# Half-frequency Fourier mixer and another order of the modulation blocks in a two-layer diffusion backbone

## The reference, cut to what matters

```python
def ada_modulation(cond, w_mod, b_mod):            # w_mod is 1024 x 6144, one for each layer
    m = jax.nn.silu(cond) @ w_mod + b_mod
    return jnp.split(m, N_MOD, axis=-1)

def fourier_mix(u):                                 # u is real: 256 tokens x 4 groups of 128 channels
    b, n, _ = u.shape
    ug = u.astype(jnp.float32).reshape(b, n, FNET_GROUPS, FNET_GROUP_DIM)
    y = jnp.fft.fft2(ug, axes=(1, 3), norm='ortho').real
    return y.reshape(b, n, FNET_WIDTH).astype(u.dtype)

def even_layer(...):
    sh1, sc1, g1, sh2, sc2, g2 = ada_modulation(c[:, None, :], mod_w, mod_b)
    h = modulate(rms_norm(x, norm_mix), sh1, sc1) @ w_in
    u, q, k, v = jnp.split(h, cuts, axis=-1)
    q = rms_norm(split_heads(q, NA_HEADS, NA_HEAD_DIM), q_gain)
    k = rms_norm(split_heads(k, NA_HEADS, NA_HEAD_DIM), k_gain)
    o_lat = jnp.concatenate([fourier_mix(u), neighbourhood_attention(q, k, v, kc, vc, rpb)], axis=-1)
    x = x + g1 * (o_lat @ w_out)
    x = x + g2 * swiglu(modulate(rms_norm(x, norm_ffn), sh2, sc2), w1, w3, w2)
```

## Time and profile before

| | us |
|---|---|
| device time, median of 3 runs | 1917.22 (1913.81 to 1921.48) |
| device time of the profiled execution | 1918.17 |
| its span, first to last instruction | 1916.0 |
| PE busy | 1820.9 (95%) |
| start of the input projection | 46.76 |
| its end, start of the transposes of q and k | 152.53 |
| start of the Fourier pass | 158.85 |
| end of the Fourier pass | 179.68 |
| start of the output projection | 267.97 |

### The profile page before, as it was taken

One profiled execution on the slowest core, in us unless ns is written; L12 is line 12 of the kernel. 1 busy time (PEld: TensorE's weight loads), 2 busy tenths in 40 slices (PEclk: granted clock), 3 DMA queues, 4 the chain that ended last, 5 costly groups with the idle time before them and its releaser, 6 DMA issues.

```text
span 1916.0 us, 25182 instructions
## 1 busy us (share of the span) xinstructions
PE 1820.9 (95%) x8938; PEld 1416.2 (74%) x8938; DVE 1262.6 (66%) x1321; ACT 1002.5 (52%) x1088; POOL 313.0 (16%) x584
## 2 busy tenths in 40 slices
PE   3999889999999989797999999999999999999998
PEld 1775444888888876465888888888888888888886
DVE  2433633433333344644998988989889899898997
ACT  3322322422222221363677767777777777776774
POOL 6888821011010224101000000000000000000000
PEclk8999999999999999897999999999999999999999
DMA  9575952032322151502699998999989999998994
GB/s 369 203 280 174 374 211 88 33 121 77 112 86 93 72 201 58 162 4 88 262 368 356 354 374 336 367 351 359 371 345 363 348 357 370 350 358 347 366 366 184
DMA packets 72373, 481.80 MB, mean 251 GB/s; under 512 B 8368, under 2 KB 11568, under 8 KB 17456
## 3 DMA queue, kind: packets, MB, share of 16 engines
q1 hardware_dynamic: 68720, 470.82, 64.7%
q0 software_dynamic: 2448, 7.61, 1.3%
q10 hardware_dynamic: 1136, 2.47, 0.4%
HBM read 473.55 MB, written 7.32 MB: 251 GB/s over the span
## 4 chain that ended last, share of the span: by engine, by line
PE 91%; DMA 4%; DVE 2%; issue 1%; ACT 1%; SPq 0%; POOL 0%; DVEq 0%; ACTq 0%
PE bank L1020 32%; PE bank L1034 16%; PE bank L752 12%; PE bank L722 4%; PE bank L605 3%; PE bank L781 3%; PE bank L769 3%; DMA ring<-in_od_mod 3%; PE bank L818 2%; PE bank L547 2%; PE bank L993 2%; DMA ring<-in_ev_mod 1%; PE bank L1003 1%; PE bank L589 1%; PE bank L571 1%
## 5 line engine op out<-in xcount | busy, mean ns | idle before, releaser
L1772 DVE TENSOR_TENSOR rest<-ring,WR 128x2048 fp32r<-128x2048 f32 x336 | 758.5, 2289 | 79.4 <-ACT WR L1344 78.6
L1344 ACT ACTIVATE WR<-ring 128x2048 fp32r<-128x2048 f32 x336 | 631.6, 1917 | 49.0 <-DMA ring<-in_experts 47.9
L1020 PE MATMUL bank<-WR,xer 128*128 128x512 f32 x1792 | 580.9, 396 | 0.7 <-DVE s5v L1933 0.7
L1020 PEld LDWEIGHTS bank<-WR,xer 128*128 128x128 f32 x1792 | 337.7, 188 | 68.7 <-issue 0.8
L1020 PE MATMUL bank<-rest,xer 128*128 128x512 f32 x896 | 350.5, 391 | 0.0
L1034 PE MATMUL bank<-WR,heTr 128*128 128x512 f32 x896 | 281.9, 392 | 0.0
L752 PE MATMUL bank<-hTr,WR 128*128 128x512 f32 x672 | 207.3, 390 | 0.0
L1034 PEld LDWEIGHTS bank<-WR,heTr 128*128 128x128 f32 x896 | 168.2, 188 | 34.2
L1020 PEld LDWEIGHTS bank<-rest,xer 128*128 128x128 f32 x896 | 169.3, 189 | 32.7
L1034 PE MATMUL bank<-rest,heTr 128*128 128x512 f32 x448 | 174.5, 389 | 0.0
L1624 DVE TENSOR_TENSOR rest<-ring,WR 128x2048 fp32r<-128x2048 f32 (+2 forms) x38 | 80.3, 2116 | 124.5 <-ACT WR L1269 124.3
(11 more groups left out here) (336 smaller groups left out, 2179.7 us busy)
## 6 DMA issues: line engine op xcount, KB each, us to landing
ring<-in_experts SPq DMA_DIRECT2D x336, 1024.0 KB, 4.8
ring<-in_ev_mod SPq DMA_DIRECT2D x24, 1024.0 KB, 7.4
ring<-in_od_mod SPq DMA_DIRECT2D x24, 1024.0 KB, 8.8
ring<-in_ffn_up SPq DMA_DIRECT2D x22, 1024.0 KB, 6.9
ring<-in_ffn_down SPq DMA_DIRECT2D x12, 768.0 KB, 5.2
ring<-in_ev_in SPq DMA_DIRECT2D x8, 1024.0 KB, 9.8
ring<-in_ev_out SPq DMA_DIRECT2D x4, 1024.0 KB, 9.9
ring<-in_od_out SPq DMA_DIRECT2D x4, 1024.0 KB, 12.9
```

The source lines that it names most:

```text
L1020: mm = pe.matmul(bank[m % 2][:, :], xer[:, i, 4 * kh + k, :], w[j][:, 512 * k:512 * k + 512], start=(kh == 0 and k == 0 and x == 0), stop= ...
L1344: act.activation(part(0, h), ring[:, h % HALVES, :], ACT.Copy).then_inc(split_hi, 1)
L1772: dve.tensor_tensor(part(1, h), ring[:, h % HALVES, :], part(0, h).bitcast(F32), ALU.subtract).then_inc(split_lo, 1)
```

## The change

The Fourier mixer computes frequencies 0 to 128 only. The token transform is 258 columns wide (129 cosines, 129 sines). The channel transform puts its two products of 129 columns side by side in one bank instead of summing them; ACT copies the second one to `TQ`, and DVE writes the sum for frequencies 0 to 128 and the difference, read backwards, for 129 to 255. POOL's head 2 waits for `four_o` = 8 (DVE's last write) instead of `four_b` = 8. The table `dft` shrinks from 1280 to 772 columns.

`norm_turn(0)` follows block 1 instead of block 2. ACT takes the squares first; it issues `s5b` and `s5c` behind them when the second half of block 1 is there, and `dft` after the modulated input. ACT's first split of `ev_in` no longer waits for `coef`.

Blocks 4 to 18, fifteen of them, stand at fixed chunks of `w_in_even()` (`UNDER_IN`), 19 and 20 between transposes of q and k, 21 in the Fourier pass, and 22 and 23 in steps 0 and 2 of the attention. The order and the slots of the loads follow. The projection uses banks 4, 5, 6 and 2, so that bank 7 is free for the odd layer's blocks. `modulation_row(1)` moves behind group 9 and `modulation_turn(1)` ahead of group 12. The splits of the third and fourth slot are issued one group later for the first half.

```diff
@@ tables @@
-LATE = 12
-         + [("in", 0), ("mod", 4), ("in", 1), ("mod", 5), ("mod", 6), ("in", 2), ("mod", 7), ("mod", 8),
-            ("in", 3), ("mod", 9), ("mod", 10), ("mod", 12), ("mod", 11)]
-         + [("mod", s) for s in range(13, 24)])
-EARLY_SLOT = [0, 1, 2, 0, 1, 0, 2, 0, 0, 1, 0, 0, 2, 0, 0, 1, 0] + [2, 1] * 5 + [2]
+         + [("in", 0), ("mod", 4), ("mod", 5), ("mod", 6), ("in", 1), ("mod", 7), ("mod", 8), ("mod", 9),
+            ("in", 2), ("mod", 10), ("mod", 11), ("mod", 12), ("mod", 13), ("in", 3)]
+         + [("mod", s) for s in range(14, 24)])
+EARLY_SLOT = [0, 1, 2, 0, 1, 2, 0, 2, 0, 2, 2, 1, 2, 1, 1, 0, 1, 0, 1, 2, 1, 2, 1, 2, 1, 2, 0, 1]
+UNDER_IN = {(0, 2): 4, (0, 3): 5, (0, 5): 6, (0, 7): 7, (5, 2): 8, (5, 7): 9, (7, 4): 10, (8, 7): 11, (9, 5): 12,
+            (10, 2): 13, (12, 0): 14, (13, 4): 15, (14, 1): 16, (14, 6): 17, (15, 3): 18}
+UNDER_TURN = {0: 19, 2: 20}
+UNDER_FOUR = {1: 21}
+UNDER_ATTN = {0: 22, 2: 23}
@@ fourier() on PE @@
-                            mm = pe.matmul(bank[4 + u % 2][:, :], hn[:, 0, 2 * s + k, g * P:(g + 1) * P],
-                                           dft[:, k * 512:(k + 1) * 512], start=(k == 0), stop=(k == 1))
+                            mm = pe.matmul(bank[4 + u % 2][:, 0:2 * HALF_F], hn[:, 0, 2 * s + k, g * P:(g + 1) * P],
+                                           dft[:, 2 * HALF_F * k:2 * HALF_F * (k + 1)], start=(k == 0), stop=(k == 1))
-                            mm = pe.matmul(bank[6 + v % 2][:, 0:SEQ], dft[:, 1024 + k * P:1024 + (k + 1) * P],
-                                           T1[:, v % 2, k * SEQ:(k + 1) * SEQ], start=(k == 0), stop=(k == 1))
+                            mm = pe.matmul(bank[(6, 2)[v % 2]][:, 256 * k:256 * k + HALF_F],
+                                           dft[:, 4 * HALF_F + k * P:4 * HALF_F + (k + 1) * P],
+                                           T1[:, v % 2, HALF_F * k:HALF_F * (k + 1)], start=True, stop=True)
@@ head of the PE program @@
-                if s == 2:
+                if s == 1:
                     norm_turn(0)
@@ ACT @@
-            act.wait_ge(half_landed[0], 16)
-            act.dma_start(tail[:, 0:512], a["s5b"]).then_inc(s5_raw, 16)
-            act.dma_start(tail[:, 512:1024], a["s5c"]).then_inc(s5_raw, 16)
-            act.dma_start(dft, a["dft"]).then_inc(dft_landed, 16)
             squares(0)
+            act.wait_ge(half_landed[3], 16)
+            act.dma_start(tail[:, 0:512], a["s5b"]).then_inc(s5_raw, 16)
+            act.dma_start(tail[:, 512:1024], a["s5c"]).then_inc(s5_raw, 16)
...
+            split_in(0)
             act.wait_ge(coef_ready, 1)
             act.wait_ge(ht_act, 4)
-            split_in(0)
...
+            act.dma_start(dft, a["dft"]).then_inc(dft_landed, 16)
             for x in range(1, 4):
                 split_in(x)
...
+                    act.wait_ge(four_b, v + 1)
+                    if v >= 2:
+                        act.wait_ge(four_o, v - 1)
+                    act.activation(TQ[:, v % 2, :], bank[(6, 2)[v % 2]][:, 256:256 + HALF_F], ACT.Copy).then_inc(four_q, 1)
@@ DVE @@
-                dve.tensor_copy(oT[:, g, s * SEQ:(s + 1) * SEQ], bank[6 + u % 2][:, 0:SEQ]).then_inc(four_o, 1)
+                dve.wait_ge(four_q, u + 1)
+                y, q, o = bank[(6, 2)[u % 2]], TQ[:, u % 2, :], oT[:, g, s * SEQ:(s + 1) * SEQ]
+                dve.tensor_tensor(o[:, 0:HALF_F], y[:, 0:HALF_F], q, ALU.add)
+                dve.tensor_tensor(o[:, HALF_F:SEQ], y[:, HALF_F - 2:0:-1], q[:, HALF_F - 2:0:-1],
+                                  ALU.subtract).then_inc(four_o, 1)
@@ POOL, head_bias() @@
                 if h == 2:
-                    pool.wait_ge(four_b, 8)
+                    pool.wait_ge(four_o, 8)
```

More of the change, by code:

```diff
@@ L86 @@
 H_EQ, H_EK, H_OQ, H_OK = range(4)
+HALF_F = SEQ // 2 + 1
 M_SH1, M_SC1, M_G1, M_SH2, M_SC2, M_G2 = range(0, 48, 8)
@@ L216, in build @@
         T1 = S[:, 4096:5120].rearrange("p (b n) -> p b n", b=2)
-        dft = S[:, 5120:6400]
+        TQ = T1[:, :, 320:320 + HALF_F]
+        dft = S[:, 5120:5120 + 4 * HALF_F + 2 * P]
         bias = [S[:, at:at + 512] for at in (0, 512, 4608, 5120)]
@@ L588, in w_in_even @@
                         for y, (i, k) in enumerate(PASSES):
-                            mm = pe.matmul(bank[4 + t][:, :], h[i], w[k], start=(c == 0 and y == 0),
+                            mm = pe.matmul(bank[IN_BANK[t]][:, :], h[i], w[k], start=(c == 0 and y == 0),
                                            stop=(c == DC - 1 and y == 2))
@@ L604, in w_in_even @@
                         for y, (i, k) in enumerate(PASSES):
-                            mm = pe.matmul(bank[4 + j % 4][:, :], h[i], w[k], start=(c == 0 and y == 0),
+                            mm = pe.matmul(bank[IN_BANK[j % 4]][:, :], h[i], w[k], start=(c == 0 and y == 0),
                                            stop=(c == DC - 1 and y == 2))
@@ L675, in attention @@
                             mm.then_inc(prob_turned, 1)
-                        if steps is EVEN_STEPS and r == 24 - LATE + 1:
+                        if steps is EVEN_STEPS and r == ROW_AT + 1:
                             modulation_turn(2)
@@ L1605, in attention @@
                                               None, ALU.mult).then_inc(prob_ready, 1)
-                        if steps is EVEN_STEPS and r == 24 - LATE:
+                        if steps is EVEN_STEPS and r == ROW_AT:
                             modulation_row(2)
```

72 lines of the change are left out of this document (44 added, 28 removed).

## The result

The changed kernel takes 1926.53 us (median of 20 runs, 1920.12 to 1931.42), the kernel before beside it 1920.16 (median of 20 runs, 1911.51 to 1925.72). The ratio is 1.0038 with a 95% interval of 1.0028 to 1.0048: 7 us slower, where the forecast was 3 us faster, and 2.5 us above the range's upper end. The profiled execution took 1926.75 us (span 1924.9), 8.6 more than the one before.

A forecast was written before the change was run, and what follows sets the result against it. It took block loads to bound the attention, with POOL's head biases as second bound right behind. F +13.6 us and the way from F to the end -16.3 gave -2.7: median 1914.5 us from 1917.22, range 1908 to 1924.

The forecast's parts named there:

- Part 1: Start of the projection: at 43.2 instead of 46.76 us, -3.5 us (-2.8 to -4.3).
- Part 2: Blocks under the projection: seven more blocks +14.8 us, waits for their loads +2.5 us (1.5 to 5).
- Part 3: Transposes and Fourier pass: blocks 19 and 20 +4.2, block 20's wait +2.1, pass -9.8, DVE's end +1.2, block 21 +2.1 us.
- F: Moment when POOL is let go for head 2 after the Fourier pass: from 179.84 to 193.4 us, +13.6.
- Part 4: From F to the output projection: 71.8 us instead of 88.1, -16.3, with POOL's chain to head 7 taking 39.1 us.
- Loads bind the projection: Rival: slower loads make blocks under the projection and among the transposes wait, adding 9 us to F; 1923.5 us, chance 0.16.
- F to the end is shorter: Rival: POOL is not the attention's bound, which ends at F + 62; 1904.5 us, chance 0.12.
- PE slows in the tail: Rival: waits for POOL leave PE at 1.2 GHz for up to eight attention steps, +9 us; 1923 us, chance 0.12.

The follow-up runs named there:

- after_pool: The changed kernel with POOL making head biases 2 to 7 in a row, ahead of tables 12 to 15: 1917.47 us, 0.9994 of the kernel before.
- late5: The changed kernel with blocks 19, 20 and 21 put back into the attention, so 19 to 23 stand in its steps 0 to 4: 1918.20 us, ratio 1.0002.
- late5_pool: late5 with POOL making head biases 2 to 7 ahead of tables 12 to 15: 1919.72 us, 1.0009 of the kernel before.
- mix2: mix2_pool with POOL's old order, four tables between its head biases as in both given kernels: 1907.44 us, 0.9935 of the kernel before.
- mix2_pool: The changed kernel with blocks 4-15 under the projection, 16-23 in the attention, block 12 loaded before ev_in's fourth slot, biases 2-7 before tables 12-15: 1903.21 us.
- after_full: The changed kernel with the full-frequency Fourier pass put back, all else kept: 1939.37 us, 1.0112 of the kernel before.
- after_bias_flat: The changed kernel with head biases loaded as 1 KB rows, same bytes and number of loads, biases not the reference's: 1922.10 us, ratio 1.0013.

## Why the prediction was wrong

Step by step, output projection at 265.2 forecast, 275.6 measured:

- **Part 1** was right: start at 42.50 (43.2 forecast).
- **Part 2, the loads under the projection**, is the term that failed. I had 2.5 us of waits (1.5 to 5) at blocks 7 and 11. These two came as forecast, 1.83 and 0.45. But measured are 6.4 us inside the projection, 3.57 of them at block 17, which the sum had as "within half a microsecond of their landing"; and the lower clock behind it, 1.7 at the block and about 1.2 in the chunks, for which the sum had nothing. I timed a block's two halves as if they had the queue to themselves or shared it with one block (landed 4.8 and 6.9 us after the first is issued); block 17's took 12.7 beside block 16's and the bias loads, which stand in POOL's timeline at 139.97 and 151.69 and were not in my working. The stretch took 132.6 us instead of 123.9; 1.9 of the 8.7 between them I can't place. The wait is no accident of one execution: in after_pool, late5 and late5_pool, which share this program, block 17 waits 2.84, 4.07 and 3.64 us, block 7 3.07, 1.68 and 1.71.
- **Part 3** was right: block 20 waited 2.24 (2.1 forecast), and a unit of the Fourier pass takes 0.87 + 0.44 or 0.45 in the chain (0.87 + 0.51 forecast), these rows:

```profile
190.33 0.87 PE bank L657 x4
191.20 0.44 PE bank L666 x4
```

- So **F** moved by 20.2, not 13.6. Part 2 alone is 8.7 over its forecast; the start, the transposes and the end behind the last product gave some 2 us back.
- **Part 4** had the mechanism right and a term too small. POOL bounds the attention (after_pool), with head 7's addition by DVE at F + 39.75 (39.1 forecast). From there to the output projection I had 32.1 us; it took 35.8, and 35.9 and 35.8 in mix2 and late5, so it isn't chance. Of the 3.7 missing, 0.5 lie ahead of the scores of step 9, and 2.2 lie between the scores of steps 9 and 15, where I took the best pace that the earlier trace rows shows for all six steps (2.62, while the same rows have 2.92 from step 13 to 15). Two of them were slower, where DVE's scalings stood beside POOL's work:

```profile
260.53 1.00 DVE L1638 TENSOR_SCALAR S<-S,rinv 128x256 f32<-128x256 f32 x1
261.63 0.94 DVE L1638 TENSOR_SCALAR S<-S,rinv 128x256 f32<-128x256 f32 x1
263.94 1.04 DVE L1638 TENSOR_SCALAR S<-S,rinv 128x256 f32<-128x256 f32 x1
265.08 1.17 DVE L1638 TENSOR_SCALAR S<-S,rinv 128x256 f32<-128x256 f32 x1
```

Alone such a scaling takes 0.35. POOL's operations of 128x512 beside them run from 259.33 to 266.10. late5 has the same four (1.18, 0.94, 1.03 and 1.16); in mix2_pool, where POOL's start at 257.85, behind the output projection, the scalings of the last steps take 0.35 to 0.44, and the scores keep the pace of 2.62. The Trainium skill's rule ("SBUF — State Buffer", "SBUF: two separate sides"), an exclusive lock for a whole instruction, fits these rows. On VectorE's side the page names operations in a two-port mode or with two inputs in SBUF; a scaling has one, and no row shows its mode, so that the lock is the cause was not shown. I had allowed it a part of 0.6 us. From the scores of step 15, which took 1.21 instead of 0.70, to the end it was 0.9 longer, at a granted clock of 0.80 from 270.0 on.
- Last, the output projection's first product ran at the lower clock for 1.2 us. I had ended the sum at its start.

The sum with the measured terms: 20.2 - 12.5 + 1.2 = +8.9, beside 8.6 between the two profiled executions.

Of the rivals, "Loads bind the projection" came nearest: 9 us for F, measured 6.6, with four of its seven blocks (7, 11, 13 and 20), but not block 17; its 1923.5 still lies 3 us under the measured median. It was worth more than 0.16: SP's 345 GB/s on average against 365 beside POOL's traffic was already in the text, and a queue used to 95% of its rate doesn't land loads in the time that one alone takes (12.7 against 6.9 us for a block). "F to the end is shorter" was wrong in the opposite direction. "PE slows in the tail" held in part: the granted clock was 0.63 from 240 to 250 us, 1.00 from 250 to 260, and 0.86 in the whole attention, where I had counted on 0.94.

The larger fault lies ahead of the terms: I priced the moves and did not ask how many pay. The table gives it. With POOL's old order the way from F to the output projection is 74.7 to 77.3 us, with two blocks in the attention (changed, after_full, after_bias_flat), with five (late5) or with eight (mix2), over values of F from 179 to 212. Only with twelve does it grow, to 84.7 and more. So four blocks out of the attention were worth 8 to 11 us there (85.7 and 88.1 against 77.3); the other six were worth at most 1.7 (77.3 against 75.6) and, with their waits, made F 20.7 later. And F has a floor of some 176 to 180, where POOL's own work ends: what the Fourier pass gave could be filled with four blocks at no cost (mix2: F 179.39, 1907.44 us), and not with more. The caution: mix2 also has other slots and another load order than the changed kernel, so its 20 us are not the number of blocks alone; nine, ten or eleven blocks were not tried. late5, which changes nothing but the place of three blocks, shows the mechanism by itself.

## What to carry to other kernels

When work is moved ahead of the point at which a second engine's chain starts, fill only the time up to the moment when that engine is ready anyway; past it, here, every microsecond moved the end, and the place that the work left gave next to nothing once the chain bound it. Before costing a moved load, list every queue that issues in those microseconds, the small loads of other engines too, and time it by loads that landed beside such traffic, not by one alone. Swapping one entry in the order of loads (a block ahead of a slot that must wait) removed a wait of 6.5 us in the trace; look for loads whose own slot is free while they stand behind one that isn't.

## What was not expected of the hardware

- A megabyte in POOL's queue, most of it bias loads of 64 KB with rows of 256 bytes, took 24.3% of the 16 engines' time in a stretch where 6.78 MB in halves of 1 MB took 75.9%: twice as much for each byte. With rows of 1 KB it was 16.2% there, with about the same number of packets (470 beside 463); where bias loads ran alone it was no cheaper (16.8% beside 14.9%, 128 packets in both), so why it was cheaper in that stretch stays open.
- Making the same biases sooner slowed the kernel before by 0.24% (0.10 to 0.38): in its trace PE waited 4.2 us more for the blocks' loads.
- Idle time of PE can be paid twice: 3.57 us without work was followed by 2.9 us lost at the lower clock. Shorter waits can do it too, though not all do: before, a block ran its 1.92 us behind a wait of 2.71 and 2.80 behind one of 2.64 (at 212.75 and 220.42 us). In late5 PE was busy for 2.73 of the 6.20 us ahead of block 21 (the wait for its load was 1.84 of the rest), and the block ran at 0.50 (windows, columns as above):

```profile
200.00:206.20 6.20, 2.73 (x8) 0.93 (x9) 5.36 (x13) 3.12 (x8) 5.81 (x10) 0.62 1.02 349
206.23:209.87 3.64, 3.64 (x18) 0.72 (x20) 2.58 (x3) 0.15 (x2) 3.64 (x5) 0.50 1.02 384
```
